# Stick breaking with a scan on VectorE whose result TensorE adds to the scores in PSUM, in a two-layer decoder step

## What is computed

```python
def stick_breaking(q, k, v, q_pos, k_pos):
    z = jnp.einsum('bthd,bshd->bhts', q, k).astype(jnp.float32) / math.sqrt(HEAD_DIM)
    mask = (k_pos[None, :] < q_pos[:, None])[None, None]
    log_1m = jnp.where(mask, jax.nn.log_sigmoid(-z), 0.0)
    after = lax.cumsum(log_1m, axis=3, reverse=True) - log_1m
    w = jnp.where(mask, jnp.exp(jax.nn.log_sigmoid(z) + after), 0.0)
    return jnp.einsum('bhts,bshd->bthd', w.astype(v.dtype), v)
```

## Time and profile before

| | us |
|---|---|
| median of three executions | 1973.53 |
| the profiled execution | 1974.06 |
| its span | 1972.3 |
| TensorE busy, matmul | 1799.3 (91%) |
| TensorE busy, weight loads | 1441.3 (73%) |
| VectorE busy | 885.2 (45%) |
| POOL busy | 534.1 (27%) |
| ScalarE busy | 508.2 (26%) |

### The profile page before, as it was taken

The page is one execution under the profiler, slowest core; times in us unless marked ns, Lnnn a source line. Parts: engine busy times, 40 slices in busy tenths (PEclk is TensorE's granted clock), DMA queues, the critical chain, the costliest instruction groups (busy, mean ns, idle before and its releaser), DMA issues. The chain is left out here.

```text
span 1972.3 us, 25345 instructions
## 1 busy us (share of the span) xinstructions
PE 1799.3 (91%) x9394; PEld 1441.3 (73%) x9394; DVE 885.2 (45%) x1717; ACT 508.2 (26%) x1305; POOL 534.1 (27%) x718
## 2 busy tenths in 40 slices
PE   6999988668899999999989998886879899999998
PEld 5888765444588888888878886644446788888887
DVE  4035426874454434343320652468554544343433
ACT  2122324345422211111111223243453222020202
POOL 0006002845132221212300330057251322121223
PEclk7999868878799999999999998687798999999999
DMA  6411403535611222222242204045273222222223
GB/s 207 171 44 43 111 22 108 190 152 199 186 64 65 86 86 86 86 86 86 86 164 73 86 1 119 13 157 207 97 267 107 86 86 85 86 86 86 86 85 129
DMA packets 107963, 210.35 MB, mean 107 GB/s; under 512 B 28160, under 2 KB 37168, under 8 KB 103360
## 3 DMA queue, kind: packets, MB, share of 16 engines
q1 hardware_dynamic: 92976, 141.58, 21.6%
q0 software_dynamic: 13824, 67.12, 9.4%
q10 hardware_dynamic: 1040, 0.00, 0.0%
HBM read 200.00 MB, written 17.06 MB: 110 GB/s over the span
## 5 line engine op out<-in xcount | busy, mean ns | idle before, releaser
L528 PE MATMUL ps<-xt,ring 128*128 128x260 f32 x1536 | 348.7, 386 | 11.1 <-DVE xt L664 11.1
L528 PEld LDWEIGHTS ps<-xt,ring 128*128 128x128 f32 x1536 | 291.1, 192 | 57.0 <-issue 12.2
L2195 ACT ACTIVATE tt<-ps 128x260 f32<-128x260 f32 x108 | 41.8, 387 | 355.9 <-PE ps L2094 236.2
L2195 ACT ACTIVATE scr<-ps 128x260 f32<-128x260 f32 x108 | 41.8, 387 | 352.2 <-PE ps L2094 227.6
L1293 PE MATMUL ps<-cst,xt 128*128 128x128 f32 x328 | 72.5, 334 | 65.2 <-ACT xt L1356 52.0
L1293 PEld LDWEIGHTS ps<-cst,xt 128*128 128x128 f32 x328 | 43.3, 167 | 107.4 <-ACT xt L1356 80.3
L606 ACT ACTIVATE tt<-ps 128x520 f32<-128x520 f32 x48 | 28.9, 603 | 289.1 <-PE ps L528 289.1
L1434 DVE TENSOR_REDUCE small<-ps 128x1 f32<-128x512 f32 (+3 forms) x128 | 56.7, 485 | 97.0 <-PE ps L1278 96.9
L1902 POOL TENSOR_TENSOR tt<-ring,tt 128x1024 f32<-128x1024 f32 x32 | 82.6, 2596 | 47.2 <-DVE scr L1705 33.6
L2140 POOL TENSOR_TENSOR x_fm<-x_fm,scr 128x260 f32<-128x260 f32 x60 | 50.6, 844 | 162.6 <-DVE scr L2289 56.3
L2140 POOL TENSOR_TENSOR x_fm<-x_fm,tt 128x260 f32<-128x260 f32 x58 | 47.9, 826 | 164.5 <-DVE tt L2350 71.2
(11 more groups left out here) (433 smaller groups left out, 3698.9 us busy)
## 6 DMA issues: line engine op xcount, KB each, us to landing
ring<-in_w_up SPq DMA_DIRECT2D x16, 2048.0 KB, 8.4
ring<-in_w_down SPq DMA_DIRECT2D x16, 2048.0 KB, 7.8
ring<-in_w_in SPq DMA_DIRECT2D x15, 2048.0 KB, 8.0
ring<-in_state_win_k SPq DMA_DIRECT2D x2, 2048.0 KB, 8.4
ring<-in_state_win_v SPq DMA_DIRECT2D x2, 2048.0 KB, 14.1
ring<-in_w_out SPq DMA_DIRECT2D x4, 1024.0 KB, 5.5
ring<-in_w_out SPq DMA_DIRECT2D x8, 512.0 KB, 8.8
out_s_win_k<-in_state_win_k SPq DMA_DIRECT2D x2, 2044.0 KB
```

The lines of the kernel that those rows point to most:

```text
L528: ins = pe.matmul(self.ps[:, 2 * (u % 2) + half, 0:H], w[:, k, f * P:(f + 1) * P], self.xtv[:, k, half * H:(half + 1) * H], start=(k == 0) ...
L2195: act.activation(tmp(u, j), bank(u, 0), ACT.Copy).then_inc(done, 1)
```

## The change

It turns the arrangement of the scores and moves the sum over the later keys from TensorE to VectorE:

- The queries are now on the partitions, and the keys of query tile qt lie at `PACK_Q[qt]`, 512, 384, 128 and 256 columns. The mask goes into PSUM ahead of the scores, so masked scores are -1e30 and their softplus is 0; the two maskings of the softplus on VectorE are gone.
- VectorE makes the negative running sum with `tensor_tensor_scan`, four per head, from the last key to the first.
- TensorE adds it to the scores in PSUM with the identity as the stationary operand, in three matmuls (`add_after`, 1280 columns).
- After Exp the weights must be turned back for the product with V: ten transposes on TensorE (`turn_weights`) and one more copy of 1280 columns on ScalarE (`copy_turned`).
- `sb_products` now has V as the stationary operand and the weights as the moving one, 512, 384, 256 and 128 columns, so its output is already transposed. ScalarE takes two heads off at once, and in `mix_and_mlp` eight of the sixteen transposes become two direct copies.
- The eight weighings of the compressed keys go from VectorE to POOL, ahead of POOL's other work.

The core of the diff:

```diff
-                def sb_cumulate(h):
-                    z, l = sb_z[h % 2], lbuf[h % 2]
-                    pe.wait_ge(l_ready, h + 1)
+                def add_after(h):
+                    pe.wait_ge(after_ready, h + 1)
+                    for a0 in range(0, PACKED, 512):
+                        n = min(512, PACKED - a0)
+                        ins = pe.matmul(sb_z[h % 2][:, a0:a0 + n], self.c("ident"), ebuf[h % 2][:, a0:a0 + n], start=False,
+                                        stop=True, skip_group_check=True)
+                    ins.then_inc(log_ready, 1)
+
+                def turn_weights(h):
+                    pe.wait_ge(w_ready, h + 1)
...
+                            ins = pe.transpose(sb_z[h % 2][:, a0:a0 + P],
+                                               lbuf[h % 2][:, PACK_Q[qt] + jb * P:PACK_Q[qt] + (jb + 1) * P], self.c("ident"))
+                    ins.then_inc(w_turned, 1)
...
                 def sb_products(h):
-                    pe.wait_ge(w_ready, h + 1)
-                    if h >= 1:
-                        pe.wait_ge(sb_o_read, h)
...
+                    pe.wait_ge(wt_copied, h + 1)
+                    if h == 2:
+                        pe.wait_ge(sb_o_read, 1)
+                    for jb in range(4):
+                        ins = pe.matmul(self.ps[(h % 2) * HD:(h % 2 + 1) * HD, 6, jb * P:SEQ],
+                                        pj[:, jb, SB_V + h * HD:SB_V + (h + 1) * HD],
+                                        ebuf[h % 2][:, PACK[jb]:PACK[jb] + SEQ - jb * P], start=(jb == 0), stop=True,
+                                        skip_group_check=True)
...
                 def softplus(h):
-                    l = lbuf[h % 2]
+                    z, l, e = sb_z[h % 2], lbuf[h % 2], ebuf[h % 2]
                     dve.wait_ge(ln_ready, h + 1)
                     if h >= 2:
-                        dve.wait_ge(cum_ready, h - 1)
...
+                        dve.wait_ge(w_turned, h - 1)
+                    dve.scalar_tensor_tensor(out=l, in0=z, scalar=0.0, in1=e, op0=ALU.max, op1=ALU.add
+                                             ).then_inc(l_ready, 1)
+                    dve.wait_ge(l_ready, h + 1)
+                    for qt in range(4):
+                        back = lambda x: x[:, PACK_Q[qt]:PACK_Q[qt] + (qt + 1) * P][:, ::-1]
+                        ins = dve.tensor_tensor_scan(back(e), back(l), back(l), 0.0, ALU.min, ALU.subtract)
+                    ins.then_inc(after_ready, 1)
```

More of the change, by code:

```diff
@@ L35 @@
 PACK = {0: 0, 1: 512, 3: 896, 2: 1024}
+PACK_Q = {3: 0, 2: 512, 0: 896, 1: 1024}
 PACKED = 1280
@@ L907, in _, with next_scores @@
+                def next_scores(h):
+                    for qt in (3, 2, 0, 1):
+                        mask(h, qt)
+                    for qt in (3, 2, 0, 1):
+                        ins = scores(h, qt)
+                    ins.then_inc(z_ready, 1)
+                for h in range(2):
+                    for qt in (3, 2, 0, 1):
+                        mask(h, qt)
+                for qt in (3, 2, 0, 1):
                     for h in range(2):
-                        ins = scores(h, jb)
-                        if jb == 2:
+                        ins = scores(h, qt)
+                        if qt == 1:
@@ L929, in _ @@
                 ret_scores(1)
-                sb_cumulate(1)
+                add_after(0)
+                add_after(1)
+                turn_weights(0)
+                ret_products(1)
                 pe.wait_ge(cmp_made, 1)
                 sb_products(0)
-                for jb in (0, 1, 3, 2):
-                    ins = scores(2, jb)
-                ins.then_inc(z_ready, 1)
-                ret_products(1)
+                next_scores(2)
                 pe.wait_ge(o_taken, 2)
                 ret_scores(2)
+                turn_weights(1)
+                ret_products(2)
                 sb_products(1)
-                for jb in (0, 1, 3, 2):
-                    ins = scores(3, jb)
-                ins.then_inc(z_ready, 1)
-                ret_products(2)
+                next_scores(3)
                 pe.wait_ge(o_taken, 3)
@@ L954, in _ @@
                 ret_scores(3)
-                sb_cumulate(2)
+                add_after(2)
                 ret_products(3)
-                sb_cumulate(3)
+                turn_weights(2)
+                add_after(3)
                 sb_products(2)
+                turn_weights(3)
                 sb_products(3)
@@ L984, in _ @@
                 weights(0)
+                copy_turned(0)
                 weights(1)
+                softplus(2)
+                copy_turned(1)
                 take_sb_output(0)
-                softplus(2)
-                take_sb_output(1)
                 softplus(3)
                 weights(2)
+                copy_turned(2)
                 weights(3)
+                copy_turned(3)
                 act.wait_ge(var_ready, 1)
@@ L2276, in _ @@
                 weight_sums(0)
[L2277 removed]
+                dve.wait_ge(t_copied, 7)
                 cat = self.xtv
```

99 lines of the change are left out of this document (41 added, 58 removed).

## The result

The changed kernel took 1943.22 us (median of 4 runs, 1939.27 to 1949.86) beside 1971.64 for the kernel before (1969.25 to 1973.89): a ratio of 0.9875, interval 0.9854 to 0.9896. Five more runs in a later comparison gave 0.9884 (0.9869 to 0.9900). The profiled execution took 1943.01 us, its span is 1941.2.

A forecast was written before the change was run, and what follows sets the result against it. TensorE, busy 91% of the span, was taken as the bound, at half clock in the stick-breaking block. From 1974.06, less 9.5 (block), 2.4 (mix) and 0.5 (to the median), came 1962 us; range 1946 to 1974.

The forecast's parts named there:

- The price of a scan: Four scan instructions per head on VectorE: 2.9 us taken, between 1.9 and 5.9, replacing two maskings of 0.8.
- the rule's 3.2: Scan estimate per head from the skill's half throughput for the built-in scan; the sum would be about 1965.
- Rivals 3 and 4: 3: scans cost 5.9 a head, 1986, chance 0.11. 4: scans run at one pass, 1.9, 1955, chance 0.08.
- Rival 3's bound of 4.3: Scan price per head from which the slower case decides: 4.7 + 1.2 gained, over four.
- Steps (a) and (b): Block's start: (a) masks, first softplus and scans, `ret_scores(1)`, to 16.0; (b) second scans, `add_after(1)`, `ret_products(1)`, to 26.85.
- Step (c): Block's middle, `sb_products(0)` through state products, to 50.1; half rate after a 0.9 wait: 4.3, 5.0, 3.6.
- rival 1: The clock holds from the block's middle on, saving 7 us a layer: 1948; chance 0.16.
- Rival 2: The clock falls earlier, at `ret_scores(2)`, and after every scan: 8 us a layer at most, 1974; chance 0.13.
- Step (d): Block's end, softplus(2) through VectorE's normalisation tail, to 81.2; TensorE waits over 2 and over 4 for scans.
- The mix: Start of the mix block: 8 of 16 transposes go, 1.8 us; 1.2 taken, 2.4 for two layers.
- POOL's cover: Eight weighing products on POOL, 4.2 us in all, covered to a few tenths before TensorE reaches `pooled`.

## Why the prediction missed

- **The price of a scan** held: 2.97 us a head for 2.9 forecast, the rule's 3.2 being the next best. Rivals 3 and 4 fall with it. (Rival 3's bound of 4.3 comes out as 4.4 from its own terms; nothing hangs on it.)
- **Steps (a) and (b)** held to 0.5 us. From the block's start, `add_after(0)` begins at 15.7 (forecast 16.0), `sb_products(0)` at 26.6 (26.85), `sb_products(1)` at 36.7 (37.2), behind a wait of 0.72 (0.9).
- **Step (c), "so from here half rate", is the step that failed.** Products, scores and sample states were put at 12.9 us and took 6.95 with the gaps between them, and the sample states end at 43.65 instead of 50.1. The rate was carried over from the 0.52 wait at 264.2 of the kernel before as if the wait made all that followed it slow. The runs show that a fall at such a wait may come or not, and that what makes it last is the short form of products(1): the change takes that away, and I carried the price of the removed form to the form put in its place. That the clock didn't fall there at all in the four traced layers of the changed kernel is partly luck; but where it did fall with the same list (weighings back on VectorE), it was back for scores and sample states, 2.42 and 1.97 behind products of 3.97, and the blocks were as long. In time this is rival 1, which got 0.16; its reason, a clock that holds, is true of these four layers and not of every run of the list. Its "against", that scores and products still fill half the rows or columns, decided nothing: the long products load only 64 columns of values, and the clock held or came back in them. Rival 2, a clock that falls earlier, did not come either.
- **Step (d)** held with the shift. `add_after(2)` begins at 48.4 (54.9 less 6.5) behind 3.25 us of waiting, at half rate as forecast (3.90 for 4.3); `add_after(3)` at 60.0 (66.7 less 6.5 is 60.2) behind 4.13, at 4.64; the next block opens at 74.8 (81.2 less 6.5 is 74.7). For two layers the block gave 21.0 instead of 9.5.
- **The mix** was mis-sized: 1.9 a layer for 1.2, all of the 1.8 of the transposes. ScalarE's two copies start with TensorE's first transpose and are done before the last one, so the 0.6 held back for them was never due.
- **POOL's cover** held. The eight products took 3.40 us for 4.2 forecast; the second four end at 227.0, before TensorE comes to them at 227.65:

```profile
225.31 1.70 POOL L1189 TENSOR_TENSOR big<-big,pos_v 128x128 f32<-128x128 f32 x4
```

- **The range.** The block and the mix alone lead to 1973.53 - 24.8 = 1949, near rival 1's 1948 and inside the range. The 1943 on record lies 6 us lower. Executions of one kernel spread by 5 to 11 us, from the sparse-attention blocks among others, and in the first pair of traces those took 3.8 us less; where the rest lies is not shown. That spread was not in the range, which ended 2 us below rival 1.

## What to carry to other kernels

A rate read from a row of the kernel before belongs to what the engine did there; where the change replaces that work, cost the step at both clocks and ask whether the cause goes with it. Look for the second gain of a change in what it makes movable: here the sums, once scans on VectorE, could run in its idle time, and the order that puts them there gave 9 us a layer where the change gave 10. Trace a kernel twice before a stretch is explained, touched or not: here single traces would have put the fall of the clock down to the form of head 0's products.

## What the runs showed of the hardware

Behind one and the same pause of 0.72 us the granted clock fell to 0.50 in eight of sixteen traced layers and held at 1.00 in the others; long or short products of head 0 ahead of it did not part the two, the time of `add_after(0)` did (4.19 to 4.35 us against 3.75 to 4.18). Once it had fallen, products of 20 records of 64 columns left it there: with both heads in the old form TensorE was busy without a gap from 262 to 274, all of it at 0.50, and the scores in that stretch, 8 records of 512 columns on 64 rows, did not bring it back either. Where 8 records of up to 512 columns on 128 rows stood in the products' place, the clock was back at their end or within the scores behind them. The Trainium skill, "TensorE: Matmul & The Clock Gate", section "HAM oscillation — how this bites in real kernels", puts the fall down to gaps in which TensorE is idle. The pause of 4.53 us agrees with that, with a fall in both layers; the pause of 0.72, with either outcome, is not decided by its length. Which property of the short records matters no run here shows.
